# A chunked delta-rule recurrence in a two-block transformer: state-free parts of all chunks in batches, one state map per chunk

## What is computed

```python
proj = h @ w_in                                     # 512 x 2816
p = p + shift_mu * (p_prev - p)                     # first 1792 columns, token shift
r, k, v, d_w, d_a, d_g = split_cols(p, ...)         # r, k, v: 8 heads of 64
decay = exp(-exp(-softplus(-(decay_base + tanh(d_w) @ decay_up)) - 0.5))
a = sigmoid(iclr_base + d_a @ iclr_up);  g = sigmoid(d_g) @ gate_up
kk = normalize(k * k_k)  # per head;     k = k * (1 + (a - 1) * k_a)
# per head, for each token t:
#   S_t = S_{t-1} diag(w_t) - (S_{t-1} kk_t)(kk_t*a_t)^T + v_t k_t^T ;  y_t = S_t r_t
y = group_norm(y) * lnx_g + lnx_b
y_a = (y + sum(r * k * r_k) * v) * g
y_b = silu(layer_norm(causal_conv31(c_val * sigmoid(c_gate))))
out = concatenate([y_a, y_b]) @ w_out
```

## Time and profile before

| | |
|---|---|
| time, median of 3 runs | 4122.06 us (4116.66 to 4128.13) |
| profiled execution | 4124.88 us, of which span 4123.1 us |
| PE busy | 3854.9 us (93%) |
| PE weight load busy | 3172.7 us (77%) |
| DVE busy | 1974.2 us (48%) |
| ACT busy | 1509.9 us (37%) |
| chain that ended last, by engine | PE 89%, DVE 6%, ACT 3% |
| mean granted clock of PE | 0.939 |

### The profile page before, as it was taken

How to read it: one execution, slowest core, us unless ns; L and a number is a source line. 1 busy time by engine, 2 the same in 40 slices (tenths; PEclk the granted TensorE clock), 3 DMA queues, 4 the chain that set the end, 5 groups by cost and what they waited for, 6 DMA issues and landing times.

```text
span 4123.1 us, 53455 instructions
## 1 busy us (share of the span) xinstructions
PE 3854.9 (93%) x20328; PEld 3172.7 (77%) x20328; DVE 1974.2 (48%) x2832; ACT 1509.9 (37%) x2305; POOL 14.4 (0%) x35
## 2 busy tenths in 40 slices
PE   8999958979999999998999999798999997899998
PEld 6887836857887888897678888577788885687887
DVE  3443485554442543323444433445577335456763
ACT  3323230124332332334443323454544335544442
POOL 0000000000000000000000000000000000000000
PEclk9999965569999999999999999899999998999999
DMA  3333200002323233222012333102222330022232
GB/s 113 97 94 90 92 22 1 1 10 78 97 94 96 81 97 97 92 89 64 1 42 92 97 96 91 39 1 68 81 97 97 94 106 6 11 92 82 97 96 93
DMA packets 84231, 296.91 MB, mean 72 GB/s; under 512 B 9520, under 2 KB 9520, under 8 KB 83696
## 3 DMA queue, kind: packets, MB, share of 16 engines
q1 hardware_dynamic: 82512, 288.24, 22.2%
q0 software_dynamic: 1568, 6.56, 0.5%
HBM read 292.66 MB, written 2.10 MB: 71 GB/s over the span
## 4 chain that ended last, share of the span: by engine, by line
PE 89%; DVE 6%; ACT 3%; issue 1%; DMA 1%; SPq 0%; DVEq 0%; ACTq 0%
PE PS L252 21%; PE PS L243 20%; PE PS L244 20%; PE PS L834 4%; PE PS L857 3%; PE PS L329 2%; PE PS L330 2%; PE PS L332 2%; PE PS L846 2%; PE PS L363 2%; PE PS L836 1%; PE PS L922 1%; PE PS L1748 1%; PE PS L1759 1%; PE PS L275 1%
## 5 line engine op out<-in xcount | busy, mean ns | idle before, releaser
L243 PE MATMUL PS<-WK_R,WHI 128*128 128x512 f32 (+1 forms) x3712 | 1440.8, 389 | 35.7 <-ACT WK_R L581 35.0
L244 PE MATMUL PS<-WK_R,WLO 128*128 128x512 f32 (+1 forms) x3712 | 1437.8, 388 | 0.0
L219 DVE TENSOR_TENSOR WLO<-RAW,WHI 128x1024 fp32r<-128x1024 f32 x563 | 689.3, 1225 | 1257.2 <-ACT WHI L215 1254.0
L215 ACT ACTIVATE WHI<-RAW 128x1024 fp32r<-128x1024 f32 x563 | 596.2, 1059 | 1025.4 <-PE PS L252 830.2
L243 PEld LDWEIGHTS PS<-WK_R,WHI 128*128 128x128 f32 x3712 | 698.8, 188 | 186.9 <-issue 39.9
L244 PEld LDWEIGHTS PS<-WK_R,WLO 128*128 128x128 f32 x3712 | 698.9, 188 | 141.2
L252 PE MATMUL PS<-H_LO,WHI 128*128 128x512 f32 x2712 | 683.0, 391 | 4.6 <-DVE H_LO L436 4.2
L252 PEld LDWEIGHTS PS<-H_LO,WHI 128*128 128x128 f32 x2712 | 508.2, 188 | 119.8 <-DVE H_LO L436 16.3
L252 PE MATMUL PS<-HID_LO,WHI 128*128 128x512 f32 x1056 | 263.2, 389 | 0.0
L252 PEld LDWEIGHTS PS<-HID_LO,WHI 128*128 128x128 f32 x1056 | 197.9, 188 | 40.9
L329 PE MATMUL PS<-WHI,WK_R 128*128 128x256 f32 (+1 forms) x736 | 191.8, 293 | 4.5 <-DVE WLO L219 4.3
(11 more groups left out here) (293 smaller groups left out, 3866.1 us busy)
## 6 DMA issues: line engine op xcount, KB each, us to landing
RAW<-in_ffn_gu SPq DMA_DIRECT2D x176, 512.0 KB, 3.6
RAW<-in_f_up SPq DMA_DIRECT2D x88, 512.0 KB, 3.4
RAW<-in_ffn_dn SPq DMA_DIRECT2D x64, 512.0 KB, 3.5
RAW<-in_c_in SPq DMA_DIRECT2D x32, 512.0 KB, 3.6
RAW<-in_f_dn SPq DMA_DIRECT2D x32, 512.0 KB, 3.5
RAW<-in_ffn_dn SPq DMA_DIRECT2D x32, 384.0 KB, 3.3
RAW<-in_a_in SPq DMA_DIRECT2D x22, 512.0 KB, 3.5
RAW<-in_b_out SPq DMA_DIRECT2D x16, 512.0 KB, 3.3
```

The costliest lines, as they stand in the source:

```text
L215: nc.scalar.activation(WHI[:, slot, :], RAW[:, slot, :], ACT.Copy).then_inc(S("w_hi"), 1)
L219: nc.vector.tensor_tensor(WLO[:, slot, :], RAW[:, slot, :], WHI[:, slot, :].bitcast(F32), ALU.subtract).then_inc(S("w_lo"), 1)
L243: pe.matmul(o, WHI[:, slot, w], hi(k), start=(first and b_ == 0), stop=False)
L244: pe.matmul(o, WLO[:, slot, w], hi(k), start=False, stop=False)
```

## The change

The mixer is rewritten; everything outside `make_mixa` stays. The panels come in a new order (`ORDER`), and all loops over panels are written out. Between panels PE does the LoRA products, head sums, the first chunk matrix and the bonus sums, and DVE the scans, the normalised key and the scaled keys and queries, as listed in `extras`. Square roots and reciprocals of head norms work on one value per token and head (`sums`, `recips`, 128 x 32), which PE spreads over the features with `head_spread`. After the panels, PE makes the other chunk matrices and 64 transposes, then for all 16 chunks at once: N times V, inverse times alpha (`W`), inverse times that (`Z`); the chunk's 64 x 64 state map `F2` and its own contribution `E2` by outer products; and the outputs that need no state. rho is replaced by rho plus a correction. The serial part per chunk is one map of the state (8 matmuls of 64 x 64), the output of the chunk by the state, and on DVE a product, an addition, one convolution tap and two additions. 44 taps are placed ahead of that part, 14 in it and the remaining 66 behind it. The inverse is made column by column: two operations per step without a reduction. The LoRA weights are loaded after the norm sum instead of after the squares, into other tiles.

The diff, cut to what carries the work:

```diff
+    ORDER = [4, 5, 6, 7, 12, 13, 18, 19, 20, 21, 14, 15, 16, 17, 0, 1, 2, 3, 8, 9, 10, 11]
...
+        for i in range(22):
+            p = panel(b, i)
...
+                env["feature_piece"](pe, p, 0, env["h_hi"], env["h_lo"], range(DT), True, True)
+            if i == 5:
...
+                    head_sums(f, KKB[f], SC[:, 4:8, :], "kk_sums")
...
+            if i == 8:
+                pe.wait_ge(S("head_recips"), 1)
+                for f in range(4):
+                    head_spread(f, KKB[f], "kk_sums")
...
+            if 6 <= i < 12:
+                lora(2 * i - 12)
+                lora(2 * i - 11)
+            if i == 16:
+                pe.wait_ge(S("factors_made"), 12)
+                gram(0, (3, 5))
+            if i == 19:
...
+                    pe.matmul(PS[:, BB[f], :], blk, SC[:, 4 + f, :], start=True, stop=True).then_inc(S("kk_sums"), 1)
+
+        pe.wait_ge(S("panel_out"), P + 22)
+        pe.wait_ge(S("factors_made"), 28)
+        gram(1, (0, 4))
...
+            turn(f, (3, 5)[f % 2])
+        pe.wait_ge(S("factors_made"), 36)
+        gram(2, (6, 7))
+        gram(3, (1, 2))
...
+        for x in range(4):
+            for h in range(NH):
+                for j in range(4):
+                    q, r, cols = x, slice(C * j, C * j + C), slice(64 * h, 64 * h + 64)
+                    mm = pe.matmul(PS[r, BA[q], cols], Nt[r, hc(h, q), :], Vt[r, q, cols], start=True, stop=True)
...
+                    mm = pe.matmul(PS[r, BB[q], cols], Tt[r, hc(h, q), :], At[r, q, cols], start=True, stop=True)
...
+                    mm = pe.matmul(PS[r, BA[q], cols], Tt[r, hc(h, q), :], NV[r, q, cols], start=True, stop=True)
...
+        def outer(half, banks, terms):
...
+                            mm = pe.matmul(PS[64 * par:64 * par + 64, banks[j], o:o + 64], l[r, q, cols], r_[r, q, cols],
...
+        outer(0, BB, [(W, Bt)]).then_inc(S("ef_done"), 1)
...
+        outer(0, BA, [(Kt, Vt), (Bt, Z)]).then_inc(S("ef_done"), 1)
...
+        def tokens(banks, l, r_, first, last):
...
+            for x in range(4):
+                if rounds[0]:
+                    pe.wait_ge(S("round_done"), rounds[0])
...
+                            mm = pe.matmul(PS[64 * par:64 * par + 64, banks[hp], o:o + C], l[r, q, 64 * h:64 * h + 64], r_[r, hc(h, q), :],
...
+        tokens(BB, W, Qt, True, True)
...
+        tokens(BB, Vt, Gt, True, False)
+        tokens(BB, Z, Qt, False, False)
+        for c in range(1, NCH):
...
+            if c > 1:
+                pe.wait_ge(S("state_ready"), 2 * (c - 1))
+            if c < NCH - 1:
...
+                        mm = pe.matmul(PS[rows, BA[2 * (c % 2) + par], 64 * hp:64 * hp + 64], F2[c // 8][rows, c % 8, hp, :], state(c)[rows, hp, :],
...
+                mm.then_inc(S("fs_done"), 1)
...
+                mm = pe.matmul(PS[rows, BB[hp], ts], state(c)[rows, hp, :], rho[rows, hp, ts], start=False, stop=(c == NCH - 1))
...
+        extras = {6: [kk_floor], 7: [kk_recip], 8: [], 9: [kk_made, lambda: decay(0)], 10: [lambda: decay(1), lambda: decay(2)],
+                  11: [lambda: decay(3), lambda: glu_made(0)], 12: [lambda: k_made((0, 1)), lambda: glu_made(1)],
+                  13: [lambda: k_made((2, 3)), lambda: glu_made(2)], 14: [a_scaled, lambda: glu_made(3)], 15: [alpha_made, beta_made],
+                  16: [lambda: at_ends(beta_end, beta)], 17: [lambda: masked(0, (3, 5), M_, "mlow")],
+                  18: [rk_made], 19: [rho_made], 20: [kappa_made], 21: [kappa_end_made]}
...
+        for s in range(C - 1):
+            m, a = C - 1 - s, s + 1
...
+            st.done(tt(o, Mp[:, s, a:C].unsqueeze(2).to_broadcast([128, m, a]), Tp[:, s, 0:a].unsqueeze(1).to_broadcast([128, m, a]), ALU.mult))
+            st.done(tt(Tp[:, a:C, 0:a], Tp[:, a:C, 0:a], o, ALU.add))
...
+        conv(44)
+        for f in range(4):
+            dve.wait_ge(S("round_done"), 4)
+            tt(rho[:, f, :], rho[:, f, :], PS[:, BB[f], :], ALU.add).then_inc(S("factors_made"), 1)
...
+            st.done(tt(d, state(c), ends[:, :, c:c + 1].to_broadcast([128, NHP, 64]), ALU.mult))
+            st.done(tt(d, d, E2[c // 8][:, c % 8], ALU.add))
+            conv(1)
+            dve.wait_ge(S("fs_done"), c)
...
+                tt(state(c + 1)[rows], d[rows], f_s, ALU.add).then_inc(S("state_ready"), 1)
```

More of the change, by code:

```diff
@@ L1673, in pe @@
+        pool.wait_ge(S("glu_made"), 4)
+        nc.gpsimd.memset(Tp, 0.0).then_inc(S("pool_set"), 1)
+        pool.wait_ge(S("pool_set"), 2)
+        nc.gpsimd.memset(flat(HID, 16, 1024)[:, 0:1024:C + 1], 1.0).then_inc(S("pool_set"), 1)
     def pe(pe, idx, n, b):
         P = b["P"]
[L1676 to L1680, removed]
@@ L1691, in pe @@
[L1691 to L1702, removed]
@@ L1703, in pe, with lora @@
[L1703 to L1710, removed]
+        def lora(k):
+            f, o = k % 4, PS[:, LORA[k % 2], :]
+            c = slice(128 * f, 128 * f + 128)
+            if k >= 2:
+                pe.wait_ge(S("lora_copied"), k - 1)
+            if k < 8:
+                rows = slice(64 * (k // 4), 64 * (k // 4) + 64)
+                mm = pe.matmul(o, updn[rows, c], lora_in[rows, :], start=True, stop=True)
+            else:
+                mm = pe.matmul(o, gup[:, c], gate_in, start=True, stop=True)
+            mm.then_inc(S("lora_done"), 1)
@@ L1711, in pe, with gram @@
+        def gram(kind, banks):
+            l, r = ((alpha, beta), (kappa, alpha), (kappa, rho), (beta, rho))[kind]
             for par in range(2):
@@ L1772, in pe, with turn @@
-        pe.wait_ge(S("y_copied"), NCH)
-        pe.wait_ge(S("state_ready"), 2 * NCH)
-        for f in range(4):
-            pe.matmul(PS[:, f, :], blk, y[:, f, :], start=True, stop=True).then_inc(S("gn_sums"), 1)
+        def turn(f, o):
+            for t in range(4):
+                src = (V_, alpha, beta_end, kappa_end)[f // 4][:, t, 128 * (f % 4):128 * (f % 4) + 128]
+                mm = pe.transpose(PS[:, o, 128 * t:128 * t + 128], src, ident)
+            mm.then_inc(S("rwkv_turned"), 1)
@@ L1789, in act @@
+        mm.then_inc(S("gn_sums"), 1)
     def act(act, idx, n, b):
@@ new lines, in beta_made, with alpha_made, chunks, at_ends @@
+        def beta_made():
+            for f in range(4):
+                tt(beta[:, f, :], kkn[:, f, :], A_[:, f, :], ALU.mult).then_inc(S("factors_made"), 1)
+            dve.wait_ge(S("factors_made"), 12)
+        def alpha_made():
+            for f in range(4):
+                tt(alpha[:, f, :], kkn[:, f, :], sg[:, f, :], ALU.mult).then_inc(S("factors_made"), 1)
+        def chunks(x, f):
+            return x[:, f, :].rearrange("p (c t) -> p c t", t=C)
+        def at_ends(dst, src):
+            dve.wait_ge(S("decays"), 13)
+            for f in range(4):
+                tt(chunks(dst, f), chunks(src, f), ends[:, f, :].unsqueeze(2).to_broadcast([128, NCH, C]), ALU.mult).then_inc(S("factors_made"), 1)
@@ L1936, in conv @@
         def conv(count):
-            for _ in range(count):
-                if done[0] == len(taps):
-                    return
+            for _ in range(min(count, len(taps) - done[0])):
                 j, f = taps[done[0]]
-                src = glu[:, f, j:j + T]
-                w = vec("cw", 4 * j + f)
+                src, w = glu[:, f, j:j + T], vec("cw", 4 * j + f)
                 if j == 0:
```

539 lines of the change are left out of this document (302 added, 237 removed).

## The result

The changed kernel takes 3999.11 us (median of 4 runs, 3997.31 to 4001.05) against 4119.92 us in the same runs: ratio 0.9706, 95% interval 0.9694 to 0.9718. The profiled execution took 3997.31 us (span 3995.5), 127.6 us less than that of before.

What follows compares the result with a forecast made beforehand. The recurrent loop was taken as bound by PE, 222.6 us. Terms for projections, batches, serial steps and close put the first output matmul 96.3 us earlier; 4124.9 became 4028.6, rounded to 4028 us, range 3990 to 4100.

Steps and rivals of the forecast that it cites:

- its 96.3 us: Whole mixer: first output matmul at 811.6 us against 907.9, 96.3 us less; the code behind it unchanged.
- Turns: PE's transposes behind the projections, around chunk matrices 2 and 3: two sets of eight turns at 1.34 us each.
- the inverse: DVE's 31 steps behind the projections: 28.1 us, masks done 46.3 us after the last projection matmul, just hidden behind PE.
- E: End of the last projection matmul, forecast at 566.3 us; later stretches are counted from it.
- Spreads: PE's spreading of head values: 64 records at 0.13 us, 8.3 us between projections; 10.7 us in the close.
- Projections, the rest: Between panels: DVE stalls 6.3 us, head sums 4.8, LoRA and bonus sums 13.7, chunk matrix 0 5.1.
- rival 4: Between the projections: all DVE's moved work shows, 39.5 us instead of 6.3, total 4062 us; chance 0.12.
- The nine groups: PE's solves, outer and token products: 256 records each at 28 ns, 7.1 us a group, 63.9 us.
- Rivals 1, 2 and 3: Nine groups don't overlap: solves, 4096 us, chance 0.07; outer and token products, 4122, 0.09; all small tiles, 4189, 0.08.
- Rounds and hand-overs: Waits in the nine groups: twelve rounds at 0.3 us, 3.6; copies 1.0; DVE's additions onto rho 2.5.
- Steps: Serial part: 14 steps at 3.0 us, 42 us; PE's 1.84 us map stands before DVE's 0.87 and hand-overs.
- Taps: DVE convolution: 44 taps hidden during PE's batches; 66 in the close unhidden, 44.5 us with PE idle.

Runs made afterwards that it cites:

- e8: Changed kernel with DVE work of panels 18 to 21 and PE's four bonus sums put behind the last panel: 4006.46 us in one run.
- e2: Changed kernel with the three solves on half their columns, same number of instructions, W copied with scale zero: 4000.61 us in one run.
- e3: Changed kernel with each of the 384 solve matmuls issued twice, same result: 4012.71 us in one run.
- e4: Changed kernel with the 14 taps of the serial steps moved ahead of them (58 there instead of 44): 3995.21 us, ratio 0.9688.
- e1: Changed kernel with 51 of the 66 closing taps moved ahead of the serial part, where DVE waits: 3957.19 us, ratio 0.9608 to before.
- e6: e5 with the masking of chunk matrix 1 moved into the inverse, ahead of its thirteenth step: 4025.91 us in one run.
- e5: Changed kernel with the eight turns of alpha and beta_end put ahead of chunk matrix 1, into PE's wait: 4000.84 us in one run.
- e9: e1 with its last 15 taps spread over the close in three fives: 3954.06 us (median of 6), ratio 0.961.

## Why the prediction was right, and where it was off

**The bound and the sum.** Where two numbers stand as "a for b" or "a (b)" below, a was measured and b forecast. PE's recurrent loop was the bound, and taking its 222.6 us off by batches gave what the sum said, on every stretch within 9.3 us. All seven differences have the same sign, so the time came out 29 below the likeliest and 9 above the range's lower end. (The sum takes its 96.3 us off the profiled execution of 4124.9, which lay 2.8 above the median.)

**Turns (-8)** are the worst single term. I read a row of eight records as one turn at 1.34 us, by the rule that a 32-bit matmul leaves two records. A transpose leaves one, since the 16 turns of four transposes leave 64 records in all: after, the sixteen records of the row at 572.39 are four turns, and eight turns take 578.78 - 572.39 = 6.4 us where 10.7 stood (and 7.6 where 11.3 stood, copy included). In the rest of that stretch chunk matrices 2 and 3 took 12.7 us for 14.2, 50 ns for a matmul, and chunk matrix 1 took 5.3 for 5.1. That PE came forward so far was possible because a second term was also too long: the inverse took 23.4 us (575.11 to 598.46) for 28.1, and DVE's masks were done at E + 41.8 instead of 46.3. At the priced length they would have held up the second solve, which began at E + 45.6.

**Spreads (-4.7).** I took 0.13 us for a record, near the 128-column transposes, and noted that halves may not overlap. 64 records took 3.71 us (L1698 at 465.73, clock 1.00), 58 ns each, half of the 117 ns that the 128-column sums cost at the same clock (L1691, 3.73 for 32): two column halves of 64 do overlap although both use all rows. The same misreading stands in the close, where the spread took 5.7 for 10.7 us and the rest 1.3 more than its terms. Why L1766's halves took 62 ns each stays open. The Trainium skill, "TensorE: Matmul & The Clock Gate", Part 3, The mechanism, would let a weight load overlap a running matmul only for another row group. These rows, with 64 loads over all 128 rows in the same 3.7 us, don't agree, as little as the earlier trace rows did.

**Projections, the rest.** Stalls on DVE between panels were 2.2 us (0.8 ahead of chunk matrix 0, 1.4 ahead of a panel), not 6.3: -4.1. Head sums 3.6 for 4.8. LoRA and bonus 15.5 for 13.7. Chunk matrix 0 took 5.1, as forecast. Of the 2.7 us that these rows leave of the 32.8, 0.5 is a later start of the first panel, and 1.7 the panel behind chunk matrix 0, a price that the sum did not have: after the gap of 2.49 us in chunk matrix 0 the granted clock was lower,

```profile
529.00:534.00 5.00, 5.00 (x18) 3.98 (x17) 0.00 (x0) 0.00 (x0) 0.00 (x0) 0.72 0.00 0
```

and the first seven of its 128x512 matmuls started 0.43 us apart instead of 0.23. e8 confirms that the cover is real; rival 4 falls.

**The nine groups (-1.4)** are the term that carried most risk. They took 7.3 to 7.5 us each (mean of each kind) for 7.1, 67.0 in all for 63.9; the waits priced with them took 2.6 for 7.1. So the stretch was hit as well as that because +3.1 and -4.5 nearly cancel, which is luck; the size of a group was not. The reason was right as well: "issue" gaps at every 128 records, whatever the tiles (e2, e3, the clocks). Rivals 1, 2 and 3 fall with it. In a burst 127 records take 1.98 us at clock 1.00. On one tile a record of 64 columns took 115 ns at clock 0.50, so an estimate for 1.00 is 58 ns, and 127 one after another would need 7.3 us. The burst took a quarter of it, and at clock 0.50 (e4) 3.63 us, a quarter of 14.6: the four row tiles worked side by side, though all four wrote one bank. The Trainium skill, "TensorEngine Tiling (Array Packing)", Gotcha 1: PSUM Pressure, would have these take turns. The trace does not agree for writes to different partitions of one bank.

**Rounds and hand-overs.** The 3.6 us for twelve waits of a round were not needed as a term, since no such wait shows beside the gaps, nor was the 1.0 at the copies. The wait for the additions onto rho was 2.62 (2.5). The wait behind panel 21 was 6.13 (6.1).

**Steps (-5.9).** 2.60 us for 3.0. The structure was the other way round from what I summed, and this step of the working is wrong although the sum came near: I put PE's map, at 1.84 us, ahead of DVE's work in one chain. The map took 1.12, since its two halves overlap, and it runs beside DVE's product, addition and tap (0.43 + 0.42 + 0.75), and these are the longer branch, with DVE's two last additions of 0.87 behind both. e4 shows it: without the tap PE's branch takes over at 2.16.

**Taps.** 43.8 for 44.5, on the path as said. What the prediction left unsaid is that they needn't be: it ends the 44 taps at 76 us behind E and the groups at 118.4, so its own numbers have DVE idle in between, and it did not price the move. e1 gives 33.3 us in the mixer for two numbers in the code.

## What to carry to other kernels

In a run of small unrolled matmuls count instructions, not columns: here 50 to 59 ns for each, whether 32 or 64 columns, at either clock. This holds where several tiles work side by side. At clock 0.50 four tiles with 64 columns nearly filled the period themselves (3.63 of 4.00 us in e4), and on one tile a record took 115 ns, far more than the supply. When work of a second engine is spread as filler, put it where that engine's own trace shows it idle (here 35 us ahead of the serial part), and not in a serial step whose other branch is shorter. To know how many instructions a row's count stands for, divide a known loop by it before using its duration.

## What the runs showed that I had not expected

**Supply of instructions.** In the nine groups bursts of 126 to 128 records start 3.4 to 4.0 us apart (3.43 from 606.48 to 609.91, 4.00 from 635.46 to 639.46 in the trace after), and the mix differs between executions: e6's nine groups had more of the long ones than e5's. After a wait of 6.13 us chunk matrix 1 ran 192 records before the first gap, and chunk matrix 0, behind a panel of long matmuls and a wait of 0.82, ran 196. So something fills up while PE takes few instructions, and a wait is not all lost time. e5 agrees; with the wait partly filled, the three chunk matrices took 19.4 us together instead of 5.3 + 12.7. The page counts 122 instruction packets of 16.4 KB (2.00 MB), 15 more than before, and e3 has one more for every 128 records added. That the gap is the wait for the next such packet is the reading that fits best; no row shows a fetch in time, so it is not shown.

**Clock after the mixer.** The same code of later layers took up to 27 us more or 7 us less, together with another granted clock: 0.71 for 0.93 in e6; in e1 0.97 for 0.93 in the 100 us that answer to 3300 to 3400 after. The whole's mean clock went from 0.956 to 0.966 with times from 3988 to 3951 for one kernel (e9). Of a change of a few us in one stage, the trace of that stage tells more than the time of the whole. What makes the clock fall in one execution and not in the next stays open.
